# Attention weights kept as one f32 copy, even and odd key tiles in two column groups of TensorE, and modulation products in four

## Chip, cores and metric

The kernel runs on one core of one Trainium2 chip. The metric is device time in microseconds (us), lower is better. The engines are TensorE (PE in the rows, PEld its weight loads), VectorE (DVE), ScalarE (ACT), GpSimd (POOL) and the DMA queues that SyncE (SP) feeds.

## What is computed

One layer of a streaming encoder, in f32, over 2048 prompt rows and 32 sample rows of width 1024: an adaptive layer norm, a projection to pooling channels and to queries, keys and values of 8 heads of 64, a multi-scale pooling, a causal stick-breaking attention, an output projection with a residual layer norm, and a SwiGLU block of inner width 2816. The change touches two parts of it:

```python
c = silu(c); m = c @ w_ada + b_ada            # (1, 1024) @ (1024, 6144), for two conditioning vectors
# attention, per head, s < t:
z = (q @ k.T) / 8
A[t, s] = sigmoid(z[t, s]) * prod_{s < j < t} (1 - sigmoid(z[t, j]))
out[t] = sum_s A[t, s] * v[s]
```

## The kernel before

Every engine runs its own instruction stream, written by hand and held together with semaphores. Products of large matrices are made of f16 high and low parts (three f16 products for one f32 product). The program's stages are the modulation and layer norm of the input, the 16 column blocks of the projection, the prompt's attention (profile time 492 to 1106 us), the output projection and sample attention, and the SwiGLU.

**Attention.** A head has ten units `UNITS` (b, kc), one for each block b of 512 queries and each block kc of 512 keys up to it, in the order (0,0), (1,1), (1,0), (2,2), (2,1), (2,0), (3,3) ... (3,0). A unit has four tiles, so there are `NTILE` = 320 tiles, numbered m. In the four diagonal units (kc = b) the tiles are 128, 256, 384 and 512 wide, in the six others 512. A tile passes through these steps, each engine at its own step of one loop over m:

- PE `scores(m + 3)`: two f16 matmuls (L1858) into one of four PSUM banks. It waits until the scan of tile m - 1 has left the bank.
- ACT `plus` (L964) makes beta, `minus` (L976) makes 1 - beta in place, both for two tiles at once.
- DVE `scan(m)` (L1410, L1413): the running product over keys, each row from where the key block to its right ended.
- POOL `product(m)` (L740): beta times the running product, which are the attention weights.
- PE `turn_weights(m - 5)`: up to four f32 transposes (L1880) that put key tile kt (0 to 3) of the unit into PSUM bank 4 or 5. It waits until tile m - 7 has been copied out.
- ACT `at_high(m - 5)` (L985) copies the turned weights as f16 (high part), and DVE `at_low(m - 6)` (L1429) writes what is left as the low part, into one of four buffers `C_AT`.
- PE `weigh(m - 7)`: an f16 matmul of the high part with the high and low values side by side, 128 columns (L1893), and one of the low part with the high values, 64 columns (L1895). Both add up over all key tiles of a query block in bank 6 or 7.
- ACT `head_low` (L999), DVE `head_out` (L1444) and POOL `head_split` (L751, L753) add the upper 64 rows of that bank to the lower and store the block's output, once for each b.

The values of each head are loaded by `load_v`, and split into parts by ACT `v_split` (L993) and DVE `v_low` (L1435), once a head. In even heads ACT `pool_high` (L1009, L1016) and DVE `pool_low` (L1455, L1459) also convert the pooling output, five pieces a head.

**Modulation.** w_ada is read in 24 pieces of 256 columns. Eight of them are multiplied at the start (L1732), eight f32 matmuls with two weight columns (`CT`, the two conditioning vectors) into two PSUM rows; DVE copies the rows out (L1212), and PE turns them (L1740). The trace shows each f32 matmul as two instructions. The other sixteen pieces are multiplied inside the attention in the same way (L1856), ahead of the scores of the first tile of units 3, 6, 10, 13 and so on (`ADA_AT`); ACT copies the rows to `MOD_ROW` (L970) and PE turns them (L1872).

## Time and profile before

| what | us |
|---|---|
| median of 3 runs | 2767.44 (2766.02 to 2767.84) |
| the profiled execution | 2765.61 |
| its span, first to last instruction | 2763.4 |
| attention stage, first scan to last scan | 494.0 to 1089.0 |
| mean granted TensorE clock | 0.984 of 2.4 GHz |

Over the whole span PE is busy 95%, DVE 59%, ACT 41% and POOL 23%, but these are means over stages with different limits. A PE time is modelled, with its latency in it: matmuls that follow each other overlap in the rows, so what one takes of PE is the distance from start to start, not its duration. The same holds in a smaller degree for DVE and ACT, where the next instruction starts about 0.1 us before the last one ends.

### The profile page before, as it was taken

Reading aid. Unit: us, or ns where it says so; the run is one execution under the profiler, and the core shown is the slowest. Engines: PE = TensorE matmul, PEld = TensorE weight load, DVE = VectorE, ACT = ScalarE, POOL = GpSimd, SP = SyncE. Lnnn points to the kernel's source line nnn. Section 1 sums busy time; section 2 is a strip of 40 time slices with the busy share of each in tenths; the row PEclk is TensorE's granted clock in tenths of the full one; section 3 lists DMA queues with packets and bytes.
Section 4 is the critical chain, followed back from the end, with each engine's and each line's share of the span. In section 5 each row is a group of like instructions: output and inputs, shape, how many; then the busy total and the mean of one; then the engine's idle time right before and its main releaser. Section 6 shows DMA issues by size and latency. Waiting matters only on the chain.

```text
span 2763.4 us, 39203 instructions
## 1 busy us (share of the span) xinstructions
PE 2622.0 (95%) x15824; PEld 1430.6 (52%) x15824; DVE 1624.7 (59%) x2084; ACT 1136.4 (41%) x1616; POOL 645.0 (23%) x865
## 2 busy tenths in 40 slices
PE   6899899899898888999999999999999999999998
PEld 3444455344344333454566664456666544999733
DVE  4647654799999999889433233544323344644455
ACT  1522232778887888224322223222222322333331
POOL 1300000466666765223211110001111000111100
PEclk9899999999999999999999999999999999999999
DMA  6225678232323110322222224522322345433462
GB/s 233 94 67 201 234 259 237 74 92 73 81 77 85 24 60 13 129 92 86 71 77 84 62 77 130 198 92 77 100 62 74 106 139 166 119 98 88 127 202 104
DMA packets 262542, 308.25 MB, mean 112 GB/s; under 512 B 27694, under 2 KB 221038, under 8 KB 256603
## 3 DMA queue, kind: packets, MB, share of 16 engines
q1 hardware_dynamic: 243354, 236.54, 27.8%
q10 hardware_dynamic: 19008, 69.21, 7.6%
q8 instruction: 125, 2.05, 0.3%
q14 instruction: 55, 0.44, 0.1%
HBM read 267.32 MB, written 38.40 MB: 111 GB/s over the span
## 4 chain that ended last, share of the span: by engine, by line
PE 73%; DVE 14%; issue 5%; ACT 3%; POOL 1%; DMA 1%; SPq 0%; POOLq 0%; DVEq 0%; ACTq 0%
PE ps L2055 34%; PE ps L2089 18%; PE ps L1767 10%; DVE work L1413 3%; PE ps L2006 3%; DVE work L1429 3%; PE ps L1856 2%; PE ps L1880 2%; PE ps L1858 1%; ACT ps L976 1%; DVE work L1410 1%; DVE work L1582 1%; PE ps L1895 1%; DMA pool_dram<-work 1%; DVE work L1288 1%
## 5 line engine op out<-in xcount | busy, mean ns | idle before, releaser
L2055 PE MATMUL ps<-hidden_t,work 128*128 128x384 f16 (+2 forms) x7392 | 946.2, 290 | 0.6 <-DVE work L1632 0.6
L2055 PEld LDWEIGHTS ps<-hidden_t,work 128*128 128x128 f16 x7392 | 646.9, 98 | 298.7 <-issue 2.4
L2089 PE MATMUL ps<-work 128*128 128x512 f16 (+1 forms) x2244 | 489.3, 379 | 0.0
L1767 PE MATMUL ps<-hidden_t,work 128*128 128x512 f16 (+1 forms) x1920 | 355.7, 343 | 12.4 <-DVE hidden_t L1180 7.7
L2089 PEld LDWEIGHTS ps<-work 128*128 128x128 f16 (+1 forms) x2244 | 215.7, 98 | 272.7 <-issue 18.0
L740 POOL TENSOR_TENSOR work<-work 128x512 f32<-128x512 f32 (+2 forms) x320 | 304.9, 955 | 200.4 <-DVE work L1413 128.7
L787 POOL TENSOR_TENSOR work<-work 128x384 f16<-128x384 f32 (+1 forms) x154 | 118.0, 766 | 934.5 <-ACT work L1076 934.5
L1629 DVE SCALAR_TENSOR_TENSOR work<-ps,col,work 128x384 f32<-128x384 f32 (+1 forms) x154 | 80.9, 525 | 431.4 <-ACT work L1074 431.3
L1638 DVE SCALAR_TENSOR_TENSOR work<-work,col 128x1024 f16<-128x1024 f32 x132 | 168.1, 1280 | 227.2 <-ACT work L1086 227.2
L1086 ACT ACTIVATE work<-work,col 128x1024 f16<-128x1024 f32 x132 | 150.8, 1147 | 290.6 <-PE ps L2089 268.9
L1074 ACT ACTIVATE work<-ps,col 128x384 f32<-128x384 f32 (+1 forms) x154 | 77.7, 505 | 450.6 <-PE ps L2055 450.6
L1767 PEld LDWEIGHTS ps<-hidden_t,work 128*128 128x128 f16 x1920 | 162.5, 98 | 193.1 <-issue 18.8
L1594 DVE SCALAR_TENSOR_TENSOR work<-work,col 128x2048 f16<-128x2048 f32 x66 | 155.0, 2349 | 155.0 <-ACT work L1065 155.0
L1413 DVE TENSOR_TENSOR_SCAN work<-ps,work 128x512 f32<-128x512 f32 x192 | 244.0, 1271 | 2.3 <-ACT ps L976 1.7
L1858 PE MATMUL ps<-work 128*128 128x512 f16 (+3 forms) x640 | 176.4, 359 | 54.0 <-DVE work L1413 40.2
L1429 DVE SCALAR_TENSOR_TENSOR work<-ps,work 128x512 f16<-128x512 f32 (+1 forms) x320 | 187.8, 587 | 28.3 <-ACT work L985 27.6
L985 ACT ACTIVATE work<-ps 128x512 f16<-128x512 f32 (+1 forms) x320 | 170.4, 532 | 70.8 <-PE ps L1880 70.3
L1880 PE MATMUL ps<-ident,work 128*128 128x128 f32 x1088 | 183.8, 285 | 13.5 <-POOL work L740 5.3
L964 ACT ACTIVATE work<-ps,col 128x1024 f32<-128x1024 f32 (+1 forms) x160 | 164.7, 1030 | 40.4 <-PE ps L1858 37.2
L1880 PEld LDWEIGHTS ps<-ident,work 128*128 128x128 f32 x1088 | 125.4, 143 | 97.3 <-DVE work L1429 56.4
L701 POOL TENSOR_TENSOR work<-work,col 128x1 f32<-128x1 f32 x68 | 40.6, 596 | 558.8 <-DVE work L1164 558.8
L2006 PE MATMUL ps<-work,hidden_t 128*128 128x512 f16 (+1 forms) x768 | 169.8, 381 | 0.0
(209 smaller groups left out, 2442.9 us busy)
## 6 DMA issues: line engine op xcount, KB each, us to landing
work<-in_w_gu SPq DMA_DIRECT2D x132, 512.0 KB, 5.0
work<-in_w_down ACTq DMA_DIRECT2D x132, 512.0 KB, 3.6
work<-in_w_ada SPq DMA_DIRECT2D x24, 1024.0 KB, 5.3
work<-in_w_gu SPq DMA_DIRECT2D x22, 1024.0 KB, 5.4
work<-in_w_down SPq DMA_DIRECT2D x11, 1024.0 KB, 5.5
work<-in_x_prompt SPq DMA_DIRECT2D x8, 1024.0 KB, 7.0
work<-in_w_in SPq DMA_DIRECT2D x16, 512.0 KB, 6.7
out<-work SPq DMA_DIRECT2D x32, 256.0 KB, 5.6
```

Source lines behind the costliest of these rows:

```text
L740: pool.tensor_tensor(a[:, 0:n], a[:, 0:n], PRJ[:, j, BLK * kc + 1:BLK * kc + n + 1], ALU.mult).then_inc(prod_set, 1)
L964: act.activation(C_A[u % 3][:, j:j + 2, 0:n], ps[:, z:z + 2, 0:n], ACT.Sigmoid, scale=c1(C_Z + 2 * (h // 2) + 1)).then_inc(be_set, 1)
L985: act.activation(C_AT[k % 4][:, 0, j0:BLK], ps[:, 4 + k % 2, j0:BLK], ACT.Identity, scale=2.0 ** TOP).then_inc(at_act, 1)
L1413: v.tensor_tensor_scan(row, ps[:, m % 4, w - 1::-1], row, PRJ[:, j, at + w:at + w + 1], ALU.mult, ALU.bypass).then_inc(scan_set, 1)
L1429: v.scalar_tensor_tensor(C_AT[k % 4][:, 1, j0:BLK], ps[:, 4 + k % 2, j0:BLK], 2.0 ** TOP, C_AT[k % 4][:, 0, j0:BLK], ALU.mult, ALU.subtrac ...
L1638: v.scalar_tensor_tensor(home[:, 1, :], E_DRAW[g % 3], c1(C_SWD), home[:, 0, :], ALU.mult, ALU.subtract).then_inc(wd_lo, 1)
L1767: mm = pe.matmul(bank(blk, n, blk), B_HL[s][:, wh * KD * P + k * P:wh * KD * P + (k + 1) * P], moving(k, xh, blk), start=(k == 0 and (wh, ...
L1858: mm = pe.matmul(ps[:, m % 4, 0:w], C_Q[e][:, qt:qt + P], C_K[e][:, half, BLK * kc:BLK * kc + w], start=(half == 0), stop=(half == 1))
L1880: mm = pe.transpose(ps[:, 4 + k % 2, j * P:(j + 1) * P], C_A[u % 3][:, j, kt * P:(kt + 1) * P], ident[:, :])
L2006: mm = pe.matmul(ps[0:rows, (2 * s if t < NT else 6) + n, :], hidden_t[:, t, k, xh, 0:rows], D_WO[k][:, wh, 512 * n:512 * (n + 1)], start= ...
L2055: mm = pe.matmul(out, E_GHL[s][:, wh, k, w, :], x, start=(k == 0 and (wh, xh) == (0, 0)), stop=(k == KD - 1 and (wh, xh) == TERMS[-1]))
L2089: mm = pe.matmul(ps[0:rows, 2 * slot + half, :], E_HID[:, j, xh, at:at + rows], E_DHL[slab_home(g)][:, wh, 512 * half:512 * (half + 1)], s ...
```

## The change

Attention: `at_high` and `at_low` become one `at_copy`, which writes the turned weights once as f32 and scales them by `C_SMIX`. ACT makes it for three key tiles in four, DVE for key tile 1 of each unit. The values are used as loaded, in f32: `v_split` and `v_low` go, and `load_v` waits for the last weighing of the head whose buffer it takes. `weigh` is one f32 matmul of 64 columns. Even key tiles go to PSUM rows 0 to 63 (the first half of TensorE's columns), odd ones to rows 64 to 127 (the second half), and PE weighs two tiles one after the other at every second step, where it weighed one at each. The first odd tile of a block starts at column 128, so a small bf16 matmul sets the 128 columns before it to zero.

Modulation: `CT` becomes 32 columns wide, of which 30 are zero. The eight products of a piece go to four column groups in turn, PSUM rows 0, 32, 64 and 96 and up. The turning becomes an f32 matmul over 128 rows with `SEL`, which also adds up the four groups.

```diff
+        CT = hidden_t[:, NT, :, 0, 64:128].bitcast(f32)
+        SEL = small[:, 24:26]
+        C_V = [w32(22576 + D * e, D).rearrange("p (i c) -> p i c", c=HD) for e in range(2)]
+        C_AT = [w32(28720 + 512 * i, 512) for i in range(4)]
+        def copied(k):
+            by_dve = (k + 3) // 4
+            return (at_dve, by_dve) if k % 4 == 1 else (at_act, k + 1 - by_dve)
...
                 if h and h + 1 < NH:
-                    sp.wait_ge(v_lo, h)
-                    load_v((h + 1) // 2, (h + 1) % 2)
                     sp.wait_ge(z_mm, 4 * NU * h)
                     load_qk((h + 1) // 2, (h + 1) % 2)
+                    sp.wait_ge(av_mm, 4 * NU * h)
+                    load_v((h + 1) // 2, (h + 1) % 2)
...
-            def at_high(k):
+            def at_copy(k):
...
+                if k == 0:
+                    act.wait_ge(mix_set, 1)
                 act.wait_ge(at_mm, k + 1)
                 if k >= 4:
                     act.wait_ge(av_mm, k - 3)
-                act.activation(C_AT[k % 4][:, 0, j0:BLK], ps[:, 4 + k % 2, j0:BLK], ACT.Identity,
-                               scale=2.0 ** TOP).then_inc(at_act, 1)
-            def v_split(h):
...
+                act.activation(C_AT[k % 4][:, j0:BLK], ps[:, 4 + k % 2, j0:BLK], ACT.Identity,
+                               scale=c1(C_SMIX)).then_inc(at_act, 1)
...
-                if 5 <= m < NTILE + 5:
-                    at_high(m - 5)
+                if 5 <= m < NTILE + 5 and m % 4 != 2:
+                    at_copy(m - 5)
...
-                v.tensor_copy(A_MROW[0:2, 256 * s:256 * (s + 1)], ps[0:2, s % 2, 0:256]).then_inc(ada_row, 1)
+                v.tensor_copy(A_MROW[:, 256 * s:256 * (s + 1)], ps[:, s % 2, 0:256]).then_inc(ada_row, 1)
...
-                v.scalar_tensor_tensor(C_AT[k % 4][:, 1, j0:BLK], ps[:, 4 + k % 2, j0:BLK], 2.0 ** TOP,
-                                       C_AT[k % 4][:, 0, j0:BLK], ALU.mult, ALU.subtract).then_inc(at_dve, 1)
-
-            def v_low(h):
...
+                if k >= 4:
+                    v.wait_ge(av_mm, k - 3)
+                v.tensor_scalar(C_AT[k % 4][:, j0:BLK], ps[:, 4 + k % 2, j0:BLK], c1(C_SMIX), None,
+                                ALU.mult).then_inc(at_dve, 1)
...
-                if 6 <= m < NTILE + 6:
-                    at_low(m - 6)
+                if 6 <= m < NTILE + 6 and m % 4 == 3:
+                    at_copy(m - 6)
...
-                    mm = pe.matmul(ps[0:2, s % 2, 0:256], CT[:, :, k], A_WADA[:, s, k, :],
-                                   start=(k == 0), stop=(k == KD - 1))
+                    at = TS * (k % 4)
+                    mm = pe.matmul(ps[at:at + TS, s % 2, 0:256], CT[:, k, :], A_WADA[:, s, k, :],
+                                   start=(k < 4), stop=(k >= 4))
...
-                mm = pe.transpose(ps[:, 2, 2 * q:2 * q + 2], A_MROW[0:2, q * P:(q + 1) * P], ident[0:2, 0:2])
+                mm = pe.matmul(ps[:, 2, 2 * q:2 * q + 2], A_MROW[:, q * P:(q + 1) * P], SEL, start=True, stop=True)
...
                 if k >= 2:
-                    pe.wait_ge(at_dve, k - 1)
+                    pe.wait_ge(*copied(k - 2))
...
             def weigh(k):
                 u, h, b, kc, kt, w = tile_of(k)
-                e = h % 2
+                e, r = h % 2, HD * (kt % 2)
                 j0 = kt * P if kc == b else 0
-                pe.wait_ge(at_dve, k + 1)
+                pe.wait_ge(*copied(k))
...
-                pe.matmul(ps[:, 6 + b % 2, j0:BLK], C_VHL[:, e, 4 * kc + kt, :], C_AT[k % 4][:, 0, j0:BLK],
-                          start=(kc == b and kt == 0), stop=(kc == 0 and kt == 3), skip_group_check=True)
-                pe.matmul(ps[0:HD, 6 + b % 2, j0:BLK], C_VHL[:, e, 4 * kc + kt, 0:HD], C_AT[k % 4][:, 1, j0:BLK],
-                          start=False, stop=(kc == 0 and kt == 3), skip_group_check=True).then_inc(av_mm, 1)
+                if kc == b and kt == 1:
+                    pe.matmul(ps[HD:P, 6 + b % 2, 0:P], C_TRI[:, 0:HD], ident_b[:, :], start=True, stop=False,
+                              skip_group_check=True)
+                pe.matmul(ps[r:r + HD, 6 + b % 2, j0:BLK], C_V[e][:, 4 * kc + kt, :], C_AT[k % 4][:, j0:BLK],
+                          start=(kc == b and kt < 2), stop=(kc == 0 and kt >= 2),
+                          skip_group_check=True).then_inc(av_mm, 1)
...
-                if m >= 7:
+                if m >= 8 and m % 2 == 0:
+                    weigh(m - 8)
                     weigh(m - 7)
```

The inner products of L1856 and the turning at L1872 change in the same way as L1732 and L1740.

PE inside a unit off the diagonal. Before, one tile and the start of the next: scores (L1858), transposes (L1880), two weighings (L1893, L1895).

```order
L1858 MATMUL ps<-work 128x512 x2
L1880 MATMUL ps<-ident,work 128x128 x4
L1893 MATMUL ps<-work 128x512
L1895 MATMUL ps<-work 64x512
L1858 MATMUL ps<-work 128x512 x2
```

After, two tiles: scores (L1842), transposes (L1865), then both tiles' weighings (L1881).

```order
L1842 MATMUL ps<-work 128x512 x2
L1865 MATMUL ps<-ident,work 128x128 x4
L1842 MATMUL ps<-work 128x512 x2
L1865 MATMUL ps<-ident,work 128x128 x4
L1881 MATMUL ps<-work 64x512 x2
```

The four f16 weighings of two tiles are replaced by two f32 ones that stand next to each other.

DVE at the end of a head. Before, a scan (L1413, L1410) and a low part (L1429) alternate.

```order
L1413 SCALAR_TENSOR_TENSOR work<-ps,work 128x512 [waits scan_set,prod_set,sg_set]
L1429 SCALAR_TENSOR_TENSOR work<-ps,work 128x512 [waits at_act]
L1410 SCALAR_TENSOR_TENSOR work<-ps,work 128x128 [waits scan_set,prod_set,sg_set]
L1429 SCALAR_TENSOR_TENSOR work<-ps,work 128x512 [waits at_act]
L1410 SCALAR_TENSOR_TENSOR work<-ps,work 128x256 [waits scan_set,prod_set,sg_set]
```

After, one copy (L1424) stands among four scans (L1406, L1403).

```order
L1406 SCALAR_TENSOR_TENSOR work<-ps,work 128x512 [waits scan_set,prod_set,sg_set] x4
L1424 TENSOR_SCALAR work<-ps,col 128x512 [waits av_mm,at_mm]
L1403 SCALAR_TENSOR_TENSOR work<-ps,work 128x128 [waits scan_set,prod_set,sg_set]
L1403 SCALAR_TENSOR_TENSOR work<-ps,work 128x256 [waits scan_set,prod_set,sg_set]
L1403 SCALAR_TENSOR_TENSOR work<-ps,work 128x384 [waits scan_set,prod_set,sg_set]
```

Three DVE instructions in four between scans are gone, and the one that stays waits for PE instead of ACT.

## Rows read from the trace of the kernel before

**Rows 1.** Busy us of each engine (instructions), clock, DMA in the attention stage.

```profile
492.00:1106.00 614.00, 541.70 (x2700) 243.70 (x2696) 565.50 (x772) 498.72 (x727) 394.08 (x510) 0.97 0.24 65
```

**Rows 2.** Groups of DVE instructions, same stretch: busy us, mean ns, idle before.

```profile
L1429 DVE SCALAR_TENSOR_TENSOR work<-ps,work 128x512 f16<-128x512 f32 x224 | 149.5, 667 | 28.3 <-ACT work L985 27.6
...
L1435 DVE SCALAR_TENSOR_TENSOR work<-work,col 128x1024 f16<-128x1024 f32 x8 | 11.1, 1393 | 0.1
```

**Rows 3.** Timeline (start us, duration us) inside units off the diagonal, head 4.

```profile
863.12 1.26 DVE L1413 TENSOR_TENSOR_SCAN work<-ps,work 128x512 f32<-128x512 f32 x1
...
864.31 0.66 DVE L1429 SCALAR_TENSOR_TENSOR work<-ps,work 128x512 f16<-128x512 f32 x1
...
864.89 1.26 DVE L1413 TENSOR_TENSOR_SCAN work<-ps,work 128x512 f32<-128x512 f32 x1
...
865.08 1.11 ACT L964 ACTIVATE work<-ps,col 128x1024 f32<-128x1024 f32 x1
...
866.10 0.59 ACT L985 ACTIVATE work<-ps 128x512 f16<-128x512 f32 x1
...
866.57 1.09 ACT L976 ACTIVATE ps<-ps,col 128x1024 f32<-128x1024 f32 x1
```

**Rows 4.** Timeline: the first scans of heads 0 to 3 and 5 to 7, and the last.

```profile
493.99 0.42 DVE L1410 TENSOR_TENSOR_SCAN work<-ps,work 128x128 f32<-128x128 f32 x1 [0.48 <-ACT ps L976]
...
576.05 0.41 DVE L1410 TENSOR_TENSOR_SCAN work<-ps,work 128x128 f32<-128x128 f32 x1
...
648.10 0.41 DVE L1410 TENSOR_TENSOR_SCAN work<-ps,work 128x128 f32<-128x128 f32 x1
...
724.82 0.41 DVE L1410 TENSOR_TENSOR_SCAN work<-ps,work 128x128 f32<-128x128 f32 x1
...
873.58 0.41 DVE L1410 TENSOR_TENSOR_SCAN work<-ps,work 128x128 f32<-128x128 f32 x1
...
944.44 0.41 DVE L1410 TENSOR_TENSOR_SCAN work<-ps,work 128x128 f32<-128x128 f32 x1
...
1022.08 0.40 DVE L1410 TENSOR_TENSOR_SCAN work<-ps,work 128x128 f32<-128x128 f32 x1
...
1089.04 1.27 DVE L1413 TENSOR_TENSOR_SCAN work<-ps,work 128x512 f32<-128x512 f32 x1
```

**Rows 5.** The chain that ended last: a modulation piece, one of sixteen.

```profile
738.68 3.62 PE ps L1856 x16
```

**Rows 6.** Timeline of PE where it hardly waits, early in head 1.

```profile
576.21 0.60 PE L1858 MATMUL ps<-work 128*128 128x512 f16 x2
576.65 0.60 PE L1880 MATMUL ps<-ident,work 128*128 128x128 f32 x4
577.09 0.38 PE L1893 MATMUL ps<-work 128*128 128x512 f16 x1
577.40 0.40 PE L1895 MATMUL ps<-work 128*64 128x512 f16 x1
577.74 0.28 PE L1858 MATMUL ps<-work 128*128 128x128 f16 x2
```

**Rows 7.** Timeline of PE in the sample attention: f32 matmuls in 32 columns.

```profile
1145.46 1.04 PE L1953 MATMUL ps<-work 64*32 64x512 f32 x2
1146.35 0.22 PE L1954 MATMUL ps<-work 64*32 64x32 f32 x2
```

**Rows 8.** Timeline of PE: modulation pieces at the start, and their turning.

```profile
15.78 29.46 PE L1732 MATMUL ps<-work,small 128*2 128x256 f32 x128 [11.93 <-DMA work<-in_w_ada]
...
47.07 1.14 PE L1740 MATMUL ps<-ident,work 2*128 2x2 f32 x16
```

**Rows 9.** Stretches: the DMA rate at the start, and a low clock after L1977.

```profile
28.00:30.00 2.00, 2.00 (x11) 0.80 (x10) 2.00 (x4) 0.00 (x0) 0.02 (x1) 1.00 1.09 347
...
1207.00:1210.00 3.00, 3.00 (x13) 1.40 (x12) 2.96 (x2) 0.00 (x0) 1.31 (x1) 0.50 0.00 0
```

58 lines of the change are left out of this document (17 added, 41 removed).

## Prediction

> **What bounds the kernel now.** The page's 40 slices show DVE at nine tenths through the attention, so I read that stage by itself. Over its 614 us DVE is busy 565 us, PE 542, ACT 499 and POOL 394 [rows 1]. The durations overlap, so I go by distances from start to start. In a unit off the diagonal two scans start 1.77 us apart (863.12 and 864.89), and between them stands one low part, 0.58 us before the next scan (864.31 to 864.89) [rows 3]. A scan thus takes 1.19 of DVE, a low part 0.58, and DVE never rests: 7.1 us for four tiles. PE's own need is less. Where it hardly waits, a tile takes 0.44 for scores, 0.44 for four transposes, 0.31 and 0.34 for the two weighings, 1.53 together [rows 6], 6.1 for four tiles. So DVE bounds these units, and PE is second. Two f16 weighings cost more than two scores (0.65 against 0.44): 0.09 is lost on going to 64 columns and 0.12 on coming back [rows 6].
>
> The heads take 82.1 (the first, with the stage's beginning), 72.1, 76.7, then 148.8 for heads 3 and 4 together, 70.9, 77.6 and 67.0 us [rows 4]. Even heads are dearer by the pooling pieces, and head 6 also has the final scales. The last two have no modulation pieces. Each of the sixteen pieces blocks PE for 3.6 us and stands on the chain [rows 5], yet head 7 is only 5.1 below head 1 with three: most of a piece lies in time that DVE's pace would take anyway.
>
> A ring also runs through a group of four tiles: a scan must end before its bank takes new scores, those go through `plus` and `minus`, and only then may the scan four tiles on start. From rows: scan 1.26, scores 0.60 [rows 6], `plus` 1.02 to the next start (865.08 to 866.10), the copy 0.47 (to 866.57), `minus` 1.09, the pair's first scan 1.19 [rows 3], and some 0.15 of hand-overs, 5.8 us. It is hidden now; nothing in the change shortens it.
>
> **The change part by part.**
>
> DVE: 240 of 320 low parts go, the other 80 become a copy of the same size, which I take at the same 0.58. That leaves 4 x 1.19 + 0.58 = 5.35 for a unit off the diagonal, where it was 7.1. The eight `v_low` (1.4 us each) go too [rows 2]. ACT: one high part in four goes, 2 x 1.02 + 2 x 0.99 + 3 x 0.47 = 5.4 for such a unit. Both fall under the ring's 5.8, so what sets the pace next is PE or the ring.
>
> PE, weighing. Nothing in the trace shows two long matmuls side by side in different columns. What it does show is an f32 matmul of 512 columns: two passes, the next work 0.89 after the first start (1145.46 to 1146.35), 0.445 a pass [rows 7]. A pair of tiles has four passes, first pass and second pass of the even tile, then of the odd one. Ends of the range: all in a row, 4 x 0.445 + 0.2 (going to 64 columns and back, rows 6) = 1.98; both tiles fully side by side, 2 x 0.445 + 0.2 = 1.09. Before, a pair cost 2 x 0.65 = 1.30. I take the value between, for this reason: PE starts its instructions in program order in every row, and a second pass adds into the same rows as the first. So of four passes only the two in the middle are neighbours in different columns and can run together: 3 x 0.445 + 0.1 (a start in the other half, as for the 0.09 in rows 6) + 0.2 = 1.63. That is 0.33 more than before, for a step meant to be side by side.
>
> First what the rows give, then the rule: rows 6 and 7 show starts in program order and 0.445 a pass. The Trainium skill, "TensorE: Matmul & The Clock Gate", Part 3, says that matmuls in different tiles overlap, but that they start and end strictly in program order; no row here has such a pair, and by that rule the pair is the 1.63 of the forecast.
>
> PE per head, with the forecast's value. Scores: six units at 1.76 and four diagonal ones at 1.1 (widths 1280 of 2048) make 15.0. Transposes likewise 14.9. Weighing: six units at 3.26; a diagonal one is 1.4 + 0.75 + 0.15 for the zero matmul = 2.3; together 28.8 (23 before). Sum 58.7. A modulation piece is eight times two passes of 0.226 now [rows 5]; with the second pass of each beside the first of the next, nine slots and seven starts in another group, 2.4 with a switch. Its bounds are 1.0 (four groups fully side by side) and 3.7. Three pieces a head make 7.2. The turning at L1872 gets two more small instructions, 0.1 each piece: nothing beside the waits there.
>
> In units where PE needs less than 5.8 the ring decides. PE works on scores of the next unit, transposes of the last and weighings of the one before that, and these mixed needs run from 4.5 (around unit (1,0)) to 6.7 (around (3,3)). Raising those below 5.8 to it adds 1.5 in a head and takes 1.5 off the pieces, since a piece fits in there. I allow 2 for waits between engines. So a head takes 68 with three pieces and 62 without. Even heads get 1.5 for pooling pieces, where 4.6 was paid (76.7 - 72.1): DVE has room for its part, ACT less. Head 6 gets 5 for the final scales, small DVE steps that stay.
>
> Sum over heads: heads 1 and 3, 72.1 to 68.3: -7.5. Heads 0, 2 and 4, 76.7 to 69.8, the first head's beginning unchanged: -20.5. Head 5, 70.9 to 64 (one piece lies in it): -6.9. Head 6, 77.6 to 68.7: -8.9. Head 7, 67.0 to 62.2: -4.8. Together -49.
>
> Start. Eight pieces hold PE without a break from 15.78 for 29.46 us, 3.7 each [rows 8]. The loads run at 347 GB/s [rows 9], so 3.0 us for a piece of 1.05 MB: pairs are there at 15.8, 21.8, 27.8 and 33.8. At 2.4 a piece PE then waits for loads, and the last pair ends at 33.8 + 4.8 = 38.6 in place of 45.2. All that follows waits for it. The turning has 32 passes at 0.07 for 16 (1.14 us [rows 8]), +1.1. I take -5 in all; bounds 0 and -8.
>
> What is moved besides. `load_v` waits on SP for the end of the last head's weighing, two units into the new head; behind it on that queue stand the modulation pieces of units 3 and 6, whose buffer is not free much earlier, and the values are needed a head later. I count 0. The C_AT buffers are freed at every second step instead of each; the copy that takes one comes four tiles on, over 5 us later, and I count 0; it is part of the 2 us of waits if not. The first products of w_o at the end share ACT and DVE with copies: -1.
>
> Sum: 2765.6 - 49 - 5 - 1 = 2710.6 for the profiled execution, whose time is 1.8 below the median of the runs shown. So about 2712.
>
> **The rivals.**
>
> *No overlap of column groups.* The four passes run in a row: 1.98 a pair, 3.7 a piece. PE per head: 29.9 + 34.4 + 11.1 = 75.4, with 2 for waits 77.4, where 72.1 was. Heads 1 and 3 lose 5.3 each, heads 0, 2 and 4 lose 2.2 each, head 5 loses 1, head 7 loses 0.8, head 6 gains 3, the start loses 1: +17, 2784. For it: no row shows an overlap, and every group of f32 passes in the trace runs one by one. Against it: these passes go to the same columns or are too short to tell. It decides from the point at which a pair takes more than about 1.85.
>
> *Full overlap.* Both tiles in 1.09, a piece in 1.0. Then the ring (5.8) and ACT (5.2 in a diagonal unit) pace a head at 58 to 60, heads gain 112 and the start 7: 2647. For it: nothing in rows. Against it: program order, as above.
> The Trainium skill, "TensorEngine Tiling (Array Packing)", Key Properties, states that tiles work independently and run loads and matmuls in parallel, with up to 2x for 64 columns. No run here shows it; by that rule the time is this rival's.
>
> *A lower clock.* After 6.8 us of f32 work in 64 columns at L1977 the granted clock is 0.50 for a stretch although PE is busy throughout [rows 9]. If the new weighings bring that about in a quarter of the stage, PE's passes there take twice as long and some 540 x 0.25 x 0.9 = 120 us come on top: 2832. Against it: the L1856 and L1732 pieces, f32 with two columns, ran at full clock [rows 9], and transposes and f16 scores stand between.
>
> **How the numbers follow.** One overlap (2712, own range 2690 to 2738, from the 2 us of waits a head being 0 to 5): 0.5. Full or nearly full overlap: 0.14. None: 0.2. Clock: 0.05. Between one overlap and none, by switches that cost more than 0.1: 0.11. The range takes in all but most of the full overlap and the clock: 2672 to 2790. A measurement tells about 0.2% from no change, 5.5 us. Faster by more: 0.5 + 0.14 + 0.08 = 0.72. Slower by more: 0.05 + 0.14 = 0.19 (the case of none reaches down to +3). Within: 0.09.
>
> **What would show it.** DVE's idle time before the scans should rise from near nothing to over 100 us in the stage. The second weighing's first pass should start 0.1 after the first one's second pass, and the pair's last 0.5 later. Scan starts should be 1.65 to 1.7 apart off the diagonal. The pieces at the start should end near 38.6. I am wrong if the four passes of a pair stand 0.445 apart (none), if all start within 0.5 (full), or if scans come faster than 1.45 apart, which would break the ring.

## Result and profile of the changed kernel

| what | before | after |
|---|---|---|
| median (range), us | 2766.73 (2765.36 to 2767.84), 4 runs | 2669.23 (2667.19 to 2672.0), 4 runs |
| profiled execution, its span | 2765.6, 2763.4 | 2669.6, 2667.4 |
| first scan to last scan | 494.0 to 1089.0 | 485.3 to 992.0 |
| mean granted clock | 0.984 | 0.984 |

The change makes the kernel faster, by 97.5 us: the ratio of the times is 0.9648, with a 95% interval of 0.9632 to 0.9665. The prediction was 2712, with a range of 2672 to 2790; the direction is right, and the gain is 1.8 times the one forecast, just outside the range.

The span is 96.0 us shorter. The first scan comes 8.7 earlier (485.31 for 493.99), the scans take 506.7 instead of 595.1 from first to last, 88.4 less, and what follows the last scan takes 1.1 more. The 88.4 is firm: a run with the same attention (the one with neighbours in the same group, below) has 506.9. The 8.7 is not: eleven profiles here have the new start of the kernel, and their first scans stand between 484.0 and 491.6, 488.0 in the mean, while three with the old start have 493.9 to 494.1. So the start is worth 6 in the mean. The first scans of heads 0, 1 and 2 and the last scan of all, from the timeline of DVE of the kernel after (start us, duration us; answers to [rows 4]):

```profile
485.31 0.42 DVE L1403 TENSOR_TENSOR_SCAN work<-ps,work 128x128 f32<-128x128 f32 x1 [0.47 <-ACT ps L979]
...
551.12 0.99 DVE L1403 TENSOR_TENSOR_SCAN work<-ps,work 128x128 f32<-128x128 f32 x2
...
612.82 0.41 DVE L1403 TENSOR_TENSOR_SCAN work<-ps,work 128x128 f32<-128x128 f32 x1
...
991.97 1.27 DVE L1406 TENSOR_TENSOR_SCAN work<-ps,work 128x512 f32<-128x512 f32 x1
```

From the same rows of every head, the heads' lengths in us (head 7 up to the start of the last scan):

| head | 0 | 1 | 2 | 3 | 4 | 5 | 6 | 7 |
|---|---|---|---|---|---|---|---|---|
| before | 82.1 | 72.1 | 76.7 | 72.1 | 76.7 | 70.9 | 77.6 | 67.0 |
| after | 65.8 | 61.7 | 63.9 | 61.7 | 63.9 | 61.6 | 66.4 | 61.5 |

Head 7, without any piece of the modulation, is now as long as heads 1 and 3 with three pieces each. Past the first head, units off the diagonal take 6.0 to 6.6 us where neither pooling pieces nor the final scales fall, and diagonal ones 5.5 to 6.3.

Busy time of each engine from first scan to last, of the kernel before and of the one after (stretch, its length, then PE, PEld, DVE, ACT and POOL busy with their instructions, clock, DMA share, GB/s; they answer to [rows 1]):

```profile
494.00:1089.00 595.00, 525.41 (x2621) 235.85 (x2621) 549.73 (x753) 487.40 (x712) 392.70 (x508) 0.98 0.24 65
```

```profile
485.00:992.00 507.00, 448.75 (x2684) 214.76 (x2684) 420.50 (x511) 468.85 (x626) 393.67 (x508) 0.99 0.27 77
```

DVE was busy 92% of that time and is now busy 83%. ACT had 82% and now has 92%, PE has 88% in both. No engine is busy throughout. The chain of what released what says the same. These are the shares of the chain by engine and line between first scan and last scan, before and then after ("issue" is time in which the engine waited for nothing that the profile shows):

```profile
by line: issue 20.2%; DVE work L1413 15.4%; DVE work L1429 13.6%; PE ps L1856 9.7%; PE ps L1880 6.7%; PE ps L1858 6.1%; DVE work L1410 5.2%; ACT ps L976 5.2%; PE ps L1895 3.8%; PE ps L1893 2.3%; DVE hidden_t L1455 2.2%; ACT work L964 1.9%; 
```

```profile
by line: DVE work L1406 14.4%; issue 13.6%; POOL work L743 11.0%; PE ps L1865 10.5%; PE ps L1842 8.8%; ACT work L967 7.8%; PE ps L1881 7.8%; ACT ps L979 7.8%; DVE work L1403 2.9%; POOL hidden_t L756 2.4%; POOL hidden_t L754 1.6%; DVE work L
```

Before, DVE's scans and low parts made a third of the chain and the modulation pieces (L1856) a tenth. After, scans (L1406) have 14%, products (L743), transposes (L1865), scores (L1842), `plus` (L967), weighings (L1881) and `minus` (L979) 8 to 11% each, and the pieces (L1840) one hundredth, which the line above cuts off.

What made it so is seen in the timeline of PE after, around one pair of weighings (L1881):

```profile
846.12 1.08 PE L1881 MATMUL ps<-work 128*64 128x512 f32 x4
847.13 0.61 PE L1842 MATMUL ps<-work 128*128 128x512 f16 x2
```

Four passes of 0.445 each [rows 7] are over, and the next scores start, 1.01 us after the first pass began. In start times of the single passes, the even tile's first pass stands at 0, the odd tile's at 0.007, and both second passes at 0.480 and 0.487. Two column groups work fully side by side. The stretches of this pair, with the busy time of L1881 alone, show it too (PE busy can't exceed the stretch, but its count in brackets shows how many passes lie in it):

```profile
846.10:846.30 0.20, 0.18 (x2) 0.19 (x4) 1.00 0.00 0
846.30:846.50 0.20, 0.20 (x2) 0.01 (x2) 1.00 0.00 0
846.58:846.70 0.12, 0.12 (x4) 0.00 (x0) 1.00 0.00 0
```

In the first half of the pair two passes are under way at once; around the change to the second ones all four are in view.

At the start of the kernel the eight pieces of the modulation go in pairs, each pair at once when its load is there (PE, start us, duration us, the wait ahead and what ended it; answers to [rows 8]):

```profile
15.70 3.64 PE L1715 MATMUL ps<-work,hidden_t 128*32 128x256 f32 x32 [11.85 <-DMA work<-in_w_ada]
...
27.65 3.42 PE L1715 MATMUL ps<-work,hidden_t 128*32 128x256 f32 x32 [2.68 <-DMA work<-in_w_ada]
...
35.09 3.43 PE L1715 MATMUL ps<-work,hidden_t 128*32 128x256 f32 x32 [4.03 <-DMA work<-in_w_ada]
...
40.26 3.63 PE L1723 MATMUL ps<-small,work 128*128 128x2 f32 x32
```

PE, which worked on them for 29.46 us without a break, now waits for every pair, and with these waits comes a lower clock. Two stretches of the start, first of the kernel before and then of the one after (the figure behind the busy times is the granted clock):

```profile
27.65:31.00 3.35, 3.35 (x17) 1.30 (x16) 2.53 (x6) 0.00 (x0) 0.64 (x3) 1.00 1.09 348
35.10:38.50 3.40, 3.40 (x17) 1.36 (x16) 0.36 (x2) 0.00 (x0) 0.00 (x0) 1.00 1.02 404
```

```profile
27.65:31.00 3.35, 3.35 (x32) 1.38 (x32) 1.24 (x2) 0.00 (x0) 0.00 (x0) 0.54 1.09 349
35.10:38.50 3.40, 3.40 (x33) 1.43 (x33) 0.43 (x1) 0.00 (x0) 0.00 (x0) 0.55 1.02 405
```

After waits of 2.7 and 4.0 us the granted clock is near its lower level, 1.2 GHz, and a pair takes 3.4, where two pieces inside the attention take 2.0. The first two pairs are as slow (3.6 and 3.3) with 1.00 in the clock's records, for which these runs show no reason; the profile of the run with short weighings, whose start is the same, has 1.93 for the second pair. The last pair ends at 38.5. The turning behind it takes 3.6 instead of 1.1 [rows 8].

### The profile page after: what moved, and what is told of

Same layout as the page of the kernel before. It is cut to its first block, busy times and chain, and to the rows that moved or that the text cites. A ratio compares the mean times of both kernels' runs of the same rounds, so it can differ in the third digit from the quotient of the medians.

```text
span 2667.4 us, 39004 instructions
## 1 busy us (share of the span) xinstructions
PE 2533.2 (95%) x15904; PEld 1408.1 (53%) x15904; DVE 1493.0 (56%) x1838; ACT 1117.4 (42%) x1528; POOL 646.8 (24%) x865
## 4 chain that ended last, share of the span: by engine, by line
PE 64%; DVE 8%; ACT 4%; POOL 3%; issue 3%; POOLq 0%; DVEq 0%; ACTq 0%
PE ps L2043 35%; PE ps L2077 18%; PE ps L1994 3%; DVE work L1406 3%; PE ps L1865 2%; POOL work L743 2%; PE ps L1881 2%; PE ps L1842 2%; ACT work L967 1%; ACT ps L979 1%; DVE work L1564 1%; DVE work L1403 1%; DVE work L1151 0%; POOL hidden_t L756 0%; DVE work L1569 0%
## 5 line engine op out<-in xcount | busy, mean ns | idle before, releaser
L743 POOL TENSOR_TENSOR work<-work 128x512 f32<-128x512 f32 (+2 forms) x320 | 306.7, 964 | 111.1 <-DVE work L1406 63.0
L1406 DVE TENSOR_TENSOR_SCAN work<-ps,work 128x512 f32<-128x512 f32 x192 | 237.4, 1270 | 34.8 <-ACT ps L979 33.8
L1842 PE MATMUL ps<-work 128*128 128x512 f16 (+3 forms) x640 | 174.0, 355 | 37.1 <-DVE work L1406 30.1
L1865 PE MATMUL ps<-ident,work 128*128 128x128 f32 x1088 | 177.9, 279 | 21.7 <-POOL work L743 17.0
L1865 PEld LDWEIGHTS ps<-ident,work 128*128 128x128 f32 x1088 | 131.2, 143 | 89.1 <-DVE work L1424 28.5
L967 ACT ACTIVATE work<-ps,col 128x1024 f32<-128x1024 f32 (+1 forms) x160 | 165.1, 1032 | 8.5 <-PE ps L1842 6.9
L979 ACT ACTIVATE ps<-ps,col 128x1024 f32<-128x1024 f32 (+1 forms) x160 | 161.5, 1009 | 2.1
L990 ACT ACTIVATE work<-ps,col 128x512 f32<-128x512 f32 (+2 forms) x240 | 148.5, 619 | 31.3 <-PE ps L1865 28.3
```

Source lines behind the costliest of these rows:

```text
L743: pool.tensor_tensor(a[:, 0:n], a[:, 0:n], PRJ[:, j, BLK * kc + 1:BLK * kc + n + 1], ALU.mult).then_inc(prod_set, 1)
L967: act.activation(C_A[u % 3][:, j:j + 2, 0:n], ps[:, z:z + 2, 0:n], ACT.Sigmoid, scale=c1(C_Z + 2 * (h // 2) + 1)).then_inc(be_set, 1)
L979: act.activation(ps[:, z:z + 2, 0:n], ps[:, z:z + 2, 0:n], ACT.Sigmoid, scale=c1(C_Z + 2 * (h // 2))).then_inc(sg_set, 1)
L1406: v.tensor_tensor_scan(row, ps[:, m % 4, w - 1::-1], row, PRJ[:, j, at + w:at + w + 1], ALU.mult, ALU.bypass).then_inc(scan_set, 1)
L1842: mm = pe.matmul(ps[:, m % 4, 0:w], C_Q[e][:, qt:qt + P], C_K[e][:, half, BLK * kc:BLK * kc + w], start=(half == 0), stop=(half == 1))
L1865: mm = pe.transpose(ps[:, 4 + k % 2, j * P:(j + 1) * P], C_A[u % 3][:, j, kt * P:(kt + 1) * P], ident[:, :])
```

## Experiments

All are measured against the kernel before, whose median in the same sessions was 2767 to 2768. Times below are medians; lengths of heads and of the scans from first to last are from the profiled execution. The latter are the finer measure for the attention, since the time of the first scan varies by up to 7.6 us between profiles with the same start. Two theories stood after the result. **Side by side**: the whole difference from the prediction is that column groups overlap fully, and everything else in its sum holds. **Something else**: the gain comes from the work taken off DVE, and the overlap is a detail. Then a second question came up: what sets the pace now.

**The modulation part alone.** The kernel before, with four column groups for the pieces and the turning with `SEL`; attention weights as before.

```diff
...
-                        pe.matmul(ps[0:2, 0, 256:512], CT[:, :, d], C_ADA[:, d, :], start=(d == 0), stop=(d == KD - 1))
+                        at = TS * (d % 4)
+                        pe.matmul(ps[at:at + TS, 0, 256:512], CT[:, d, :], C_ADA[:, d, :], start=(d < 4), stop=(d >= 4))
```

> The kernel before with the modulation products in four column groups and the turning with SEL, its attention left as it was. Theory (a piece costs about 1.1 us of PE instead of 3.6, and the scans are then held by DVE alone): the three pieces of a head stop costing their 4.5 us, so -1.5 x 16 = -24 in the attention, and -4 to -9 at the start: 2733 to 2740. Rival (DVE bounds the stage, so a shorter piece is hidden and only the start gains): 2758 to 2763.

Measured: 2739.11 (2738.81 to 2744.68), ratio 0.9900 [0.9883, 0.9916], 28 us less than before. First scan 5.0 earlier, first to last scan 576.7 (595.1). The stretch of the attention:

```profile
489.00:1066.00 577.00, 495.37 (x2653) 230.97 (x2653) 548.81 (x754) 490.20 (x713) 393.52 (x508) 0.96 0.25 67
```

```profile
by line: issue 23.6%; DVE work L1417 18.6%; DVE work L1433 15.6%; POOL work L741 5.9%; ACT ps L977 5.4%; PE ps L1887 5.1%; PE ps L1864 5.0%; DVE work L1414 4.1%; DVE hidden_t L1459 2.8%; PE ps L1902 2.5%; DVE work L1448 2.0%; PE ps L1900 1.
```

PE is busy 30 us less than before the change, and DVE has the same 549 us, now 95% of the time, with its scans (L1417, L1414) and low parts (L1433) first among the engines in the chain: heads 1 and 3 shrink to 68.5 and 69.3 us (72.1 before), and DVE's work stops them there. So of the 2.6 us (3.6 to 1.0) that each of sixteen pieces gives back, 1.15 reach the end (18.4 / 16), as the prediction argued for the old pieces: most of a piece lay in time that DVE took anyway. The 1.15 is rather low: this profiled execution was 5.6 us above the median, at a granted clock of 0.87 in head 6. Heads 1 and 2, at 1.00 throughout, give 1.2 and 1.3 a piece.

**The attention part alone.** The kernel after, with pieces and turning as before.

```diff
...
-                        at = TS * (d % 4)
-                        pe.matmul(ps[at:at + TS, 0, 256:512], CT[:, d, :], C_ADA[:, d, :], start=(d < 4), stop=(d >= 4))
+                        pe.matmul(ps[0:2, 0, 256:512], CT[:, :, d], C_ADA[:, d, :], start=(d == 0), stop=(d == KD - 1))
```

> The changed kernel with its modulation as before: two PSUM rows, 3.6 us a piece. Theory (the two parts share little): the attention part is worth 97 less what e1 shows, some -65: 2700. Rival (the parts need each other, since with a faster attention each piece of 3.6 us is paid in full): 16 x 2.5 + 8 above the changed kernel, 2717 or more.

Measured: 2707.62 (2705.05 to 2709.16), ratio 0.9786 [0.9771, 0.9800], 60 us less than before and 38 more than the whole change, between the two forecasts. The shares of the chain between first and last scan, by line:

```profile
by line: PE ps L1858 12.7%; PE ps L1874 12.6%; PE ps L1836 11.9%; PE ps L1834 10.6%; DVE work L1402 10.1%; issue 9.9%; POOL work L742 7.7%; ACT ps L978 4.7%; ACT work L966 3.9%; DVE work L1399 3.7%; DVE work L1420 1.8%; POOL hidden_t L755 1
```

The long pieces (L1834) have their tenth of the chain again, and heads 1 and 3 take 66.6 where the one without pieces takes 61.5. First to last scan is 535.8, 29.1 more than with short pieces, so a long piece costs 1.8 here of its 2.6, against 1.15 in the kernel that DVE bounds. The two parts give 28 and 60, together 88, where the whole change gives 98: each is worth more with the other in place.

**Both tiles of a pair in the same half.** The kernel after, but odd tiles go to rows 0 to 63 as the even ones do, and the upper half is set to zero once a block.

```diff
-                e, r = h % 2, HD * (kt % 2)
+                e, r = h % 2, 0
...
-                if kc == b and kt == 1:
-                    pe.matmul(ps[HD:P, 6 + b % 2, 0:P], C_TRI[:, 0:HD], ident_b[:, :], start=True, stop=False,
+                if kc == b and kt == 0:
+                    pe.matmul(ps[HD:P, 6 + b % 2, :], C_TRI[:, 0:HD], C_TRI[:, 0:BLK], start=True, stop=True,
...
```

> The changed kernel with odd key tiles in the same 64 columns as the even ones; a bf16 matmul of zeros over all 512 columns sets the upper half once a block. Theory (the two f32 weighings of a pair run side by side only in different columns): a pair takes 1.98 us of PE instead of 1.09, four passes 0.445 apart, a unit off the diagonal 7.4 instead of 6.2, in all +50 to +70: 2720 to 2740. Rival (they overlap for another reason, or PE has that much room): within 10 of 2669.

Measured: 2726.67 (2 runs), ratio 0.9855 [0.9836, 0.9875]: 57 us lost of the 98. PE around the same kind of pair:

```profile
839.24 1.93 PE L1881 MATMUL ps<-work 128*64 128x512 f32 x4
841.10 0.50 PE L1842 MATMUL ps<-work 128*128 128x384 f16 x2
```

1.86 us to the next scores instead of 1.01, with the passes at 0, 0.480, 0.910 and 1.339. Shares of the chain:

```profile
by line: PE ps L1881 34.2%; PE ps L1842 20.8%; PE ps L1865 18.6%; issue 4.7%; DVE work L1406 4.4%; ACT work L967 2.6%; ACT ps L979 2.6%; POOL work L743 2.2%; ACT work L997 1.8%; PE ps L1840 1.4%; PE ps L1856 1.0%; PE ps L1879 0.8%; DVE work
```

PE is now three quarters of the chain, a third of it weighings. With PE as the bound its heads can be held against the prediction's sum for PE: with 1.98 a pair and 1.1 a piece it is 29.9 + 34.4 + 3.3 + 2 for waits = 69.6 for heads 1 and 3, and they measure 69.6. The match to a tenth is partly luck, since the 2 for waits was an allowance, and the even heads, for which the sum has 1.5 more, measure 70.2. But no term of it is far off: a pair in one half is 1.86 and 0.09 on going to 64 columns, 1.95.

**No overlap anywhere.** The last two edits together: the weights copied once in f32 and the 320 low and high parts gone, but no two column groups ever side by side.

> e3 and e2 together: both tiles of a pair in the same 64 columns, and the modulation products in two rows as before. Nothing of PE's f32 work can run side by side, so this is the prediction's rival without overlap, built. The prediction's sum gave 2784 for it. From the runs: 2727 (e3) + 16 pieces x 2.6 us paid in full + 8 at the start = 2776. Rival (room elsewhere hides a good part of the pieces, as it did before the change): 2727 + 38, the price of the pieces in e2, = 2765.

Measured: 2767.16 (8 runs), ratio 0.9993 [0.9983, 1.0004], the time of the kernel before. The stretch of the attention and the shares of its chain:

```profile
492.00:1089.00 597.00, 578.70 (x2663) 269.11 (x2660) 432.60 (x516) 470.56 (x630) 392.66 (x510) 0.99 0.23 65
```

```profile
by line: PE ps L1874 34.0%; PE ps L1836 19.6%; PE ps L1858 18.0%; PE ps L1834 9.5%; DVE work L1402 5.0%; issue 3.8%; ACT ps L978 1.3%; PE ps L1872 1.1%; DVE hidden_t L1439 1.0%; ACT work L996 0.9%; ACT work L966 0.7%; DVE work L1420 0.6%; P
```

This settles the first question. DVE is busy 117 us less than before (433 for 550), and nothing of it reaches the end, because f32 weighings (L1874), scores, transposes and pieces (L1834) on PE make four fifths of the chain: PE is busy 53 us more than before (579 for 525). In this kernel the f32 weighings that take work off DVE load PE by as much as that is worth, and the overlap takes this load away. A kernel with DVE relieved and PE left alone was not run.

**Neighbours in the same group.** The eight products of a piece go to column groups 0, 0, 1, 1, 2, 2, 3, 3 instead of 0, 1, 2, 3, 0, 1, 2, 3. If PE keeps program order between groups, only the border from one group to the next can overlap.

```diff
...
-                        at = TS * (d % 4)
-                        pe.matmul(ps[at:at + TS, 0, 256:512], CT[:, d, :], C_ADA[:, d, :], start=(d < 4), stop=(d >= 4))
+                        at = TS * (d // 2)
+                        pe.matmul(ps[at:at + TS, 0, 256:512], CT[:, d, :], C_ADA[:, d, :], start=(d % 2 == 0), stop=(d % 2 == 1))
```

> The changed kernel with the eight products of a modulation piece in the order 0, 0, 1, 1, 2, 2, 3, 3 of column groups in place of 0, 1, 2, 3, 0, 1, 2, 3. If matmuls start strictly in program order and only their passes are interleaved, each second product of a group holds up the next group: five steps of two passes, 2.3 us a piece instead of 1.1, in all +10 to +20. If each column group goes through its own work without regard to the others, a piece stays at 1.1 and the time within 3 of 2669.

Measured: 2670.98 (2670.02 to 2673.12), ratio 0.9655 [0.9641, 0.9670], the time of the kernel after. A piece (L1840) takes 1.02 to the next scores, 1.00 in the kernel after:

```profile
587.47 1.09 PE L1840 MATMUL ps<-work,hidden_t 128*32 128x256 f32 x16
588.49 0.28 PE L1842 MATMUL ps<-work 128*128 128x128 f16 x2
```

The four groups' first passes start at 0, 0.013, 0.026 and 0.039, so the matmul of group 1 starts while the second matmul of group 0, which stands ahead of it in the program, has not begun (it starts at 0.456). Within these eight products the order of the groups in the program doesn't matter.

**One tile at each step.** The kernel after, halves kept, but `weigh` at every step. Between two weighings now stand scores and transposes over all columns.

```diff
-                if m >= 8 and m % 2 == 0:
-                    weigh(m - 8)
+                if m >= 7:
                     weigh(m - 7)
```

> The changed kernel with one tile weighed at each step, scores and transposes between the even and the odd one, still in two halves of the columns. If a weighing in half of the columns runs beside nothing but a weighing in the other half, each costs 0.89 + 0.2 alone, 2.18 a pair, more than e3's 1.98: 2735 to 2755. If it could also run beside the full-width work: near 2669.

Measured: 2753.75 (2 runs), ratio 0.9947 [0.9927, 0.9967]: 84 of the 98 us are lost, more than with both tiles in one half. PE in a unit off the diagonal:

```profile
851.68 1.07 PE L1881 MATMUL ps<-work 128*64 128x512 f32 x2
852.68 0.60 PE L1842 MATMUL ps<-work 128*128 128x512 f16 x2
853.13 0.60 PE L1865 MATMUL ps<-ident,work 128*128 128x128 f32 x4
```

One tile takes 1.00 to the next scores; two took 1.01. The different half is worth nothing when full-width work stands between, and leaving 64 columns is paid once a tile instead of once a pair.

**What sets the pace now.** The rest looks for it. The prediction had named the ring (scan, scores, `plus`, `minus`, scan: 5.8 us for four tiles) and ACT. If one resource alone were the bound, as DVE was before and PE was with no overlap, relief there would come through in full. The next run frees the ring of one copy of ACT, which stands between `plus` and `minus`, by putting it behind `minus`.

```diff
-                if 5 <= m < NTILE + 5 and m % 4 != 2:
+                if m % 2 == 1 and 7 <= m < NTILE + 7 and (m - 6) % 4 != 1:
+                    at_copy(m - 6)
+                if m % 2 == 1 and 5 <= m < NTILE + 5:
                     at_copy(m - 5)
```

> The changed kernel with ScalarE's copy of key tile 3 moved from between `plus` and `minus` to behind `minus`. The same instructions, so ScalarE has as much to do. If the ring (scan, scores, plus, minus, scan) sets the pace, it is 0.6 shorter in every second pair, about -2.5 a head: 2645 to 2655. If ScalarE's sum of work sets it: 2665 to 2673.

Measured: 2674.68 (2670.51 to 2676.28), ratio 0.9659 [0.9645, 0.9674], no gain: from first to last scan it takes 3.8 more. The last unit of a head falls from 6.18 to 5.72, by 0.46, about the 0.47 that the copy took of the ring, so there the ring seems to set the pace. But unit (1,1) rises from 5.67 to 6.72. Its weights are copied later, and PE waits for these copies there (0.22 and 0.25 us before its turnings and transposes); how that makes 1.05 was not followed up.

**Two copies a unit on DVE.** DVE takes both odd key tiles.

```diff
-            by_dve = (k + 3) // 4
-            return (at_dve, by_dve) if k % 4 == 1 else (at_act, k + 1 - by_dve)
+            by_dve = (k + 1) // 2
+            return (at_dve, by_dve) if k % 2 == 1 else (at_act, k + 1 - by_dve)
...
```

> The changed kernel with VectorE copying both odd key tiles (1 and 3) and ScalarE the even ones. No copy stands between `plus` and `minus`, and ScalarE has 0.6 a unit less; VectorE comes to 4 x 1.19 + 2 x 0.65 = 6.1 a unit, as much as a unit takes now. If ScalarE or the ring was the bound and VectorE stays under: 2645 to 2660. If VectorE takes their place: 2665 to 2680.

Measured: 2669.45 (2667.67 to 2674.07), ratio 0.9646 [0.9630, 0.9662], the time of the kernel after. Busy times over about one head (547 to 608.7), of after and then of this run:

```profile
547.00:608.70 61.70, 57.36 (x368) 27.96 (x360) 50.30 (x58) 57.75 (x79) 48.60 (x65) 1.00 0.33 86
```

```profile
547.00:608.70 61.70, 57.88 (x366) 28.32 (x368) 55.36 (x68) 55.08 (x69) 49.40 (x65) 1.00 0.32 86
```

ACT (fourth busy time) gives 2.7 us away and DVE (third) takes 5.1. Odd heads get 0.4 to 0.7 shorter, heads 0 and 6 get 0.9 and 1.6 longer, where DVE also has the stage's beginning and the final scales. ACT's load alone isn't the bound either, as far as a run can tell that gives DVE more work at the same time.

**Four that leave work out.** Each makes one step smaller, to learn what that step is worth. In the first ACT copies only the upper 256 columns off the diagonal, and weighing reads those twice:

```diff
-                act.activation(C_AT[k % 4][:, j0:BLK], ps[:, 4 + k % 2, j0:BLK], ACT.Identity,
+                c0 = BLK // 2 if kc != b else j0
+                act.activation(C_AT[k % 4][:, c0:BLK], ps[:, 4 + k % 2, c0:BLK], ACT.Identity,
...
```

> The changed kernel, where ScalarE copies only the upper 256 columns of each tile off the diagonal, and the weighing reads those twice: the attention's result is not the reference's, PE's work is the same, ScalarE has about 0.24 x 18 = 4.3 us a head less. If ScalarE holds the pace (by its sum, or because plus must wait for copies): -3 to -4 a head, 2637 to 2645. If the bare ring does, in which one of two copies stands: -10, 2659. If PE's order does: within 3 of 2669.

Measured: 2664.49 (2660.82 to 2668.43), ratio 0.9627 [0.9612, 0.9641], 5 less than after, between two of the forecasts. In the second, tiles off the diagonal are weighed for the upper 256 columns only, so that PE has less:

```diff
+                if kc != b:
+                    j0 = BLK // 2
```

> The changed kernel, where a tile off the diagonal is weighed for its upper 256 columns only, so its share of the other 256 is missing from the result. PE has 2 x 0.213 = 0.43 us a pair less, 5.1 a head, and nothing else changes. If the weighing, which stands between the scores of a pair in PE's order, holds the pace: -2 to -4 a head, 2640 to 2655. If ScalarE or the ring does: 2663 to 2672.

Measured: 2665.46 (2662.78 to 2671.18), ratio 0.9636 [0.9618, 0.9653], 4 less. In the third, `plus` writes only the upper 256 columns off the diagonal, which shortens both ACT and the ring:

```diff
-                act.activation(C_A[u % 3][:, j:j + 2, 0:n], ps[:, z:z + 2, 0:n], ACT.Sigmoid,
+                n0 = BLK // 2 if kc != b and u >= 3 else 0
+                act.activation(C_A[u % 3][:, j:j + 2, n0:n], ps[:, z:z + 2, n0:n], ACT.Sigmoid,
```

> The changed kernel, where plus writes only the upper 256 of 512 columns of each tile off the diagonal from the third unit on; the lower ones keep old values, so the attention's result is not the reference's. ScalarE has about 0.43 x 12 = 5 us a head less, as much as e9 and e10 took from ScalarE and PE, but every bit of it lies inside the ring (scan, scores, plus, minus, scan), one plus for each turn of four tiles. If the ring sets the pace: -0.43 x 6 = -2.6 a head, about -20, 2645 to 2653. If only the amount of ScalarE's work counts: as e9, 2660 to 2668.

Measured: 2661.14 (2659.15 to 2664.47), ratio 0.9622 [0.9606, 0.9638], 8 less. In the fourth, `head_split` on POOL stores two of four token tiles of a block:

```diff
-                st = C_ST[b % 2][r, :].rearrange("p (i t) -> p i t", t=P)
-                dst = [hidden_t[r, 4 * b:4 * b + 4, 4 + h // 2, half, :] for half in range(2)]
+                st = C_ST[b % 2][r, 0:BLK // 2].rearrange("p (i t) -> p i t", t=P)
+                dst = [hidden_t[r, 4 * b:4 * b + 2, 4 + h // 2, half, :] for half in range(2)]
```

> The changed kernel, where GpSimd's head_split stores only two of the four token tiles of each block, so half of the attention's output is missing. GpSimd has 0.3 + 0.5 = 0.8 us less for each of four blocks, 3.3 a head. The chain of waits of the changed kernel goes through product and head_split, whose delay of the transposes also delays the weighing and with it the scores behind it on PE. If that is the path that is left: -1.5 to -3 a head, 2645 to 2657. If it only takes its turn with the ring, as ScalarE's copies and PE's weighing did (e9, e10): 2660 to 2668.

Measured: 2663.08 (2659.88 to 2664.23), ratio 0.9617 [0.9601, 0.9633], 6 less. The same stretch of one head in the third of them:

```profile
547.00:608.70 61.70, 58.09 (x374) 29.18 (x374) 51.47 (x59) 53.64 (x79) 49.81 (x66) 1.00 0.32 86
```

The first and third of them relieve ACT, the second PE and the fourth POOL. On the medians they give 4 to 8 us, for the first two no more than the spread of the runs. The scans from first to last, 506.7 in the kernel after, tell them apart: 502.5, 503.3, 495.6 and 496.4. So less copying and less weighing give 0.5 and 0.4 us a head, and a shorter `plus` and a shorter `head_split` 1.4 and 1.3. In this last row ACT has 4.1 us less of work than in the kernel after, and heads 1 to 5 are 1.3 to 1.7 shorter. So neither ACT nor PE nor POOL sets the pace by itself. That no single engine does is not shown: none of the runs makes the scans on DVE shorter, which have the largest share of the chain after. A piece of the chain of the kernel after shows how they take turns (start us, us, what):

```profile
586.36 1.09 POOL work L743
...
587.51 0.61 POOL hidden_t L754
...
588.20 1.16 POOL hidden_t L756
...
589.43 1.10 POOL work L743
...
590.58 0.65 PE ps L1865 x4
591.23 0.43 PE ps L1842 x2
...
592.10 1.01 PE ps L1881 x4
593.11 0.54 PE ps L1842 x2
...
594.71 1.11 ACT work L967
...
596.27 1.11 ACT ps L979
```

At the end of a block POOL does `head_split` (L754, L756) between two products (L743); the transposes wait for the late product, the scores stand behind the transposes in PE's order, and `plus` and `minus` wait for the scores. Halving `head_split` brings unit (3,3) from 6.2 or 6.8 to 5.5 or 5.7, and past the first head unit (2,2) down by 0.2 to 0.7, but (2,0) in heads 0, 2 and 4 rises from 7.2 to 8.3. How such a delay is passed on from unit to unit, and which of these couplings is the last one, these runs leave open.

## Where the prediction was right and where it was wrong

**The step that failed** is "PE starts its instructions in program order in every row", and with it the price of a pair. The sum took the four passes as four separate steps that start in the program's order, which leaves one overlap: 1.63 a pair. Measured are 1.01 from first pass to next work, with 0.09 on going to 64 columns 1.10, which is the lower bound of the sum (1.09). An f32 matmul is one instruction of the program that makes two passes, and each column group works through its own: the odd tile's first pass starts 0.007 after the even tile's, ahead of the even tile's second pass. The rows that I took for evidence all show matmuls that share columns, for which the order does hold, also in the run with one half (0, 0.480, 0.910, 1.339). They said nothing on different columns, and the two ends of the range (1.09 and 1.98) should have stood with chances nearer to each other than 0.5 for a value between and 0.14 for the lower end. The sign that the prediction named for full overlap, all four starts within 0.5, is what the trace shows (0.487).

The Trainium skill, "TensorE: Matmul & The Clock Gate", Part 3, has matmuls in different tiles start and end in program order. The run with neighbours in the same group doesn't agree: by that rule groups 0, 0, 1, 1 could overlap only where one group follows another, and they took 1.02 a piece against 1.00. "TensorEngine Tiling (Array Packing)", Key Properties, of the same skill, says that tiles work independently, and its Overview has up to 2x for 64 columns; the trace agrees (1.86 against 1.01).

**The piece of the modulation** failed by the same step: 2.4 forecast, 1.0 measured, again the lower bound. The 2.4 doesn't follow from its own terms either: nine slots of 0.226, seven starts in another group at the 0.1 used for the pair and the switch of 0.2 make 2.9.

**PE's sum otherwise** held, as the run with one half shows: 69.6 for heads 1 and 3, with a pair at 1.98. Repriced with 1.1 for a full pair and 1.0 a piece, PE needs 29.9 for scores and transposes, 6 x 2.2 + 4 x 1.9 = 20.8 for weighings (1.9 by the widths of a diagonal unit) and 3.0 for pieces, 54 a head, and the heads take 61.7: PE is no longer the bound, which the chain confirms.

**DVE bounds the kernel before** is borne out, and the way it is seen is worth a look: with the modulation part alone DVE's busy time stays 549 and the time falls by 28 only. It is not shown by a run that relieves DVE alone. That DVE isn't busy throughout after the change was right also: its idle time rises from 45 us (595 - 550), which the prediction called near nothing, to 86 (507 - 421) between the first scan and the last. That is below the 100 given as the sign to look for, because the stage is 39 us shorter than the forecast had it (88 for 49), with the same work on DVE in it.

**The rival of full overlap** (2647) was the right mechanism and 22 us too low. It had heads at 58 to 60, by the ring's 5.8 and ACT. They are 61.5 to 64, and 66 for the first and for head 6. Two terms were too small: ACT's new copy takes 0.69 where the high part took 0.59 [rows 3], and DVE's 0.73 where the low part took 0.67 [rows 2]:

```profile
L990 ACT ACTIVATE work<-ps,col 128x512 f32<-128x512 f32 x176 | 121.8, 692 | 28.9 <-PE ps L1865 27.6
L1424 DVE TENSOR_SCALAR work<-ps,col 128x512 f32<-128x512 f32 x48 | 34.8, 726 | 0.0
L997 ACT ACTIVATE work<-ps 64x512 f32<-64x512 f32 x32 | 19.0, 594 | 3.8 <-PE ps L1881 3.0
```

The sum took a copy on ACT at the price of a high part; 0.1 more for each of three in a unit is up to 3 us a head. The 0.1 isn't the f32: L997 (`head_low`) also writes 512 columns as f32 from PSUM, in 0.59, and so does L923 over all 128 rows. It reads no column of scales, which the new copy does (`col` in its row) and the high part, scaled by a constant, didn't. The rest is in the turns that engines wait for each other. The allowance for these, 2 us a head, was in the forecast's sum for PE but not in this rival's. Past the first head no unit off the diagonal is below 6.0, so none undercuts the ring's 5.8.

**The rival of no overlap** (2784) was tried as a kernel and gave 2767.2. It decides from about 1.85 a pair, it said. Counted as the prediction counts, a pair in one half takes 1.95 (1.86 and 0.09), and at that price the kernel is as fast as before, so break-even was placed 0.1 low. Heads 1 and 3 were 76.5 where it had 77.4, but the even ones were 76.5 too, where it had 78.9 (76.7 + 2.2), and the first 77.1 for 84.3: with PE as the bound the pooling pieces and the stage's beginning cost nothing more.

**The clock** stayed (0.984 in both, 0.98 and 0.99 in the attention), as expected. What the prediction left out is the start, where PE now waits between pairs and 0.54 was granted.

**The start**: the last pair of pieces ends at 38.5 (38.6 forecast), bounded by loads as argued, but the match is luck: the pair began 1.3 later than forecast (35.1 for 33.8) and took 3.4 instead of 4.8, since two pieces need 2.0 inside the attention, not 4.8, but met a granted clock of 0.55 here. The turning took 2.5 more, not 1.1, and even so DVE's product on the modulation came 4.3 earlier (43.93 for 48.25). The first scan comes 8.7 earlier in this profile, and 6 in the mean of those with the new start, so the 5 of the forecast was about right. Why it varies by 7.6 between them was not followed up.

**Taken as nothing**: the wait of `load_v`, the C_AT buffers. No DMA wait stands in the attention's chain after, and the pace is set elsewhere; they weren't tried by themselves. The 1 us for the products of w_o isn't seen: what follows the last scan took 1.1 more, within the 1673.8 to 1677.4 that it takes over all profiles.

## What to carry to other kernels

When an added operation has a form that no row shows, give the two ends of its price (here a pair in 1.09 or in 1.98 us) their own chances, and take no value between them that rests on a rule which the rows show only for another form. Work taken off the bounding engine is worth what the second engine lets through: here 117 us off DVE gave nothing while PE's f32 passes ran in a row, and the whole change 98 once they ran side by side. Put matmuls for different columns right next to each other in the program, and don't expect much from the next relief once the chain is spread over four engines: 3 to 5 us a head off ACT, PE or POOL gave 0.4 to 1.4. Where PE comes to wait between short bursts, as at the start here, look at the granted clock before pricing the next burst.

## What the runs showed of the hardware

- Two f32 matmuls of 512 columns in different halves of TensorE's columns take 1.01 us together, 1.86 in the same half. Eight f32 products of 256 columns take 1.0 us in four groups of 32 columns, 3.6 one after the other in the same two columns.
- A column group doesn't wait for an earlier matmul of another group that hasn't begun: the order 0, 0, 1, 1, 2, 2, 3, 3 costs 1.02 and 0, 1, 2, 3 twice 1.00.
- Work over all columns between two such matmuls ends the gain: one tile then takes 1.00 to the next scores, as much as two.
- At the start, where PE waits 2.7 and 4.0 us ahead of a burst, the granted clock in it is 0.54 and 0.55, and 16 such products take 3.4 instead of 2.0.
- Turning with a matmul over 128 rows takes 0.11 a pass (3.63 for 32, at a granted clock of 1.00), where transposes over two rows take 0.07 (1.14 for 16) [rows 8].
- ScalarE copies 512 columns from PSUM in 0.59, to f16 (L985, [rows 3]) and to f32 (L997) alike, and in 0.69 with a scale that it reads from a column (L990).
